# The output stage of an RWKV block: the bonus moved into the scan, the head norm from one root

## The reference, cut to what matters

```python
ym = jnp.mean(y, -1, keepdims=True)                    # per token and head
yv = jnp.mean(jnp.square(y - ym), -1, keepdims=True)
y = ((y - ym) * lax.rsqrt(yv + RW_LNX_EPS)).reshape(B, L, D) * lnx_g + lnx_b
kd = kf[None] * (1.0 + (a - 1.0) * k_a)                # a = sigmoid(a0 + la), both directions
kdh = (kd[0] + kd[1]).reshape(B, L, H, N)
bonus = jnp.sum(rh * kdh * r_k, -1, keepdims=True) * v
out = ((y + bonus.reshape(B, L, D)) * g)
return jnp.einsum('bld,de->ble', out, w_o)
```

## Time and profile before

| | us |
|---|---|
| median of 3 runs | 3148.36 (3147.19 to 3151.6) |
| profiled execution, its own time | 3148.75 |
| its span, first to last instruction | 3146.9 |
| TensorE busy | 2713.0 (86%) |
| VectorE busy | 2072.8 (66%) |
| ScalarE busy | 1583.4 (50%) |
| GpSimd busy | 436.3 (14%) |
| scan, in the span | 673 to 1020 |
| output stage up to the first matmul of `rw_o` | 1021 to 1116 |

### The profile page before, as it was taken

One profiled execution on the slowest core, in us unless ns is written; L12 is line 12 of the kernel. 1 busy time (PEld: TensorE's weight loads), 2 busy tenths in 40 slices (PEclk: granted clock), 3 DMA queues, 4 the chain that ended last, 5 costly groups with the idle time before them and its releaser, 6 DMA issues.

```text
span 3146.9 us, 58272 instructions
## 1 busy us (share of the span) xinstructions
PE 2713.0 (86%) x25152; PEld 2497.2 (79%) x25152; DVE 2072.8 (66%) x3070; ACT 1583.4 (50%) x2567; POOL 436.3 (14%) x271
## 2 busy tenths in 40 slices
PE   7868995848999468999999999999485788887898
PEld 7538995738999258999999999999483588886898
DVE  4664336774322457999999999999545567346683
ACT  3334433444111426777777777777343355344452
POOL 2002431111000110000000000000041134221242
PEclk9758997857988678999999999999787699988999
DMA  5103451200000126999999999999131134431353
GB/s 217 45 17 115 171 186 48 82 24 3 4 4 6 72 83 227 359 341 342 357 341 352 346 337 369 334 352 357 68 127 58 41 140 169 148 136 59 128 179 117
DMA packets 83209, 539.38 MB, mean 171 GB/s; under 512 B 9488, under 2 KB 9488, under 8 KB 38912
## 3 DMA queue, kind: packets, MB, share of 16 engines
q1 hardware_dynamic: 82368, 530.99, 45.9%
q0 software_dynamic: 576, 4.58, 0.4%
HBM read 534.49 MB, written 1.05 MB: 170 GB/s over the span
## 4 chain that ended last, share of the span: by engine, by line
PE 70%; DVE 19%; ACT 8%; issue 1%; DMA 1%; POOL 1%; DVEq 0%; SPq 0%; ACTq 0%; POOLq 0%
PE ps L557 18%; PE ps L558 17%; PE ps L559 17%; DVE sl L512 2%; ACT sh L505 2%; PE ps L1255 2%; DVE arena_conv L2596 2%; PE ps L563 2%; DVE xl L553 1%; PE ps L602 1%; PE ps L1259 1%; ACT xh L548 1%; PE ps L1248 1%; PE ps L1223 1%; PE ps L1706 1%
## 5 line engine op out<-in xcount | busy, mean ns | idle before, releaser
L1926 DVE TENSOR_TENSOR sl<-ring,sh 128x1024 fp32r<-128x1024 f32 x613 | 735.0, 1219 | 29.9 <-ACT sh L1884 18.8
L557 PE MATMUL ps<-xh,sh 128*128 128x256 f32 (+1 forms) x1888 | 574.5, 304 | 134.2 <-DVE xl L553 89.9
L1884 ACT ACTIVATE sh<-ring 128x1024 fp32r<-128x1024 f32 x613 | 630.4, 1053 | 3.1 <-DVE xl L1766 1.9
L557 PE MATMUL ps<-sh,xh 128*128 128x256 f32 (+2 forms) x2012 | 594.5, 295 | 13.6 <-POOL sl L519 6.0
L558 PE MATMUL ps<-sl,xh 128*128 128x256 f32 (+2 forms) x2012 | 574.9, 286 | 0.0
L559 PE MATMUL ps<-sh,xl 128*128 128x256 f32 (+2 forms) x2012 | 574.4, 286 | 0.0
L558 PE MATMUL ps<-xl,sh 128*128 128x256 f32 (+1 forms) x1888 | 562.1, 298 | 0.0
L559 PE MATMUL ps<-xh,sl 128*128 128x256 f32 (+1 forms) x1888 | 558.4, 296 | 0.0
L519 POOL TENSOR_TENSOR sl<-ring,sh 128x1024 fp32r<-128x1024 f32 (+3 forms) x111 | 273.6, 2465 | 1953.0 <-ACT sh L505 1892.5
L557 PEld LDWEIGHTS ps<-xh,sh 128*128 128x128 f32 x1888 | 379.6, 201 | 158.3 <-DVE xl L553 102.1
L505 ACT ACTIVATE sh<-ring 128x1024 fp32r<-128x1024 f32 (+1 forms) x345 | 342.3, 1021 | 182.6 <-PE ps L559 163.1
(11 more groups left out here) (514 smaller groups left out, 4436.2 us busy)
## 6 DMA issues: line engine op xcount, KB each, us to landing
ring<-ws_d SPq DMA_DIRECT2D x229, 1024.0 KB, 7.2
ring<-ws_d SPq DMA_DIRECT2D x80, 1536.0 KB, 6.4
ring<-ws_d SPq DMA_DIRECT2D x226, 512.0 KB, 6.8
ring<-ws_d SPq DMA_DIRECT2D x24, 1408.0 KB, 6.0
ring<-ws_d SPq DMA_DIRECT2D x4, 1256.0 KB, 5.4
ring<-ws_d SPq DMA_DIRECT2D x2, 1088.0 KB, 5.0
scan_t<-scn_d POOLq DMA_DIRECT2D x1, 1824.0 KB, 7.7
arena<-ow_d POOLq DMA_DIRECT2D x1, 1536.0 KB, 12.1
```

What stands on the lines that cost most here:

```text
L557: e.matmul(out, ah, bh, start=start, stop=False)
L1884: e.activation(out, raw(u)[:, a:z], ACT.Copy).then_inc(*af.on("high", u, i))
L1926: e.tensor_tensor(l, raw(u)[:, a:z], f32(h), SUB).then_inc(s_fd if i < 2 else s_fp, 1)
```

## The change

The bonus leaves the output stage. It becomes a third generator of the scan, on every engine, which joins after the second direction's set-up and two further rounds; each of its eight tiles takes four rounds: a2's two matmuls and two sigmoids, GpSimd's two operations, VectorE's two products and TensorE's head sum, and VectorE's product with v. It reads a2's weights from the scan's constants, so `ow_d` is 1 MB, and writes into `KK`, whose content is used up by then (`VV = KK`). In the output stage the mean is taken off by one matmul with I - ones/64 (`centre`); ScalarE squares out of PSUM, VectorE writes the centred values times the gain; eight matmuls with 16 columns (`heads64`) sum the squares of all 16 heads into 16 rows of one bank; one addition, one root and one reciprocal on 16 rows follow; then for each tile the gate's matmuls, and two matmuls (K = 16, 64 columns each) that spread two heads' scales over their 64 partitions, and on VectorE scale, bias plus bonus, gate, and the low part of the tile before. TensorE waits for `ow_d` only ahead of the first gate. The constants grow by 158 columns. The loops over `staged(8, 5)` in the four output programs, which are printed above, are taken out.

```diff
+    c.append(("centre", 128, lambda _: (np.eye(128) - blk / 64).astype(f)))
+    head_of = (np.arange(30)[None, :] - 14 == p[:, None] // 64).astype(f)
+    c.append(("heads64", 30, lambda _: head_of / f(64)))
...
 def out_weights():
     return [("g2", D, lambda inp: inp["rw_g2"][0, 0:128]),
-            ("g2b", D, lambda inp: inp["rw_g2"][0, 128:160]),
-            ("a2", D, lambda inp: np.reshape(inp["rw_a2"][0], (128, D)))]
+            ("g2b", D, lambda inp: inp["rw_g2"][0, 128:160])]
...
         PREPARE = 6
-
-        def streams(steps):
+        VV, va1 = KK, HW
+        def streams(steps, bonus):
             runs = [steps(n) for n in range(2)]
             for _ in range(PREPARE):
                 next(runs[0])
+            for _ in range(PREPARE + 2):
+                for g in runs:
+                    next(g)
+            runs.append(bonus())
             while runs:
                 runs = [g for g in runs if next(g, "end") != "end"]
...
+            def bonus():
+                for k in range(8):
+                    for n in range(2):
+                        b, free = psum.take(("out a", n, k))
+                        w.wait_ge(*free)
+                        e.matmul(PS[:, b, 0:T0], sn("a2")[64 * n:64 * n + 64, 128 * k:128 * k + 128], HA[64 * n:64 * n + 64, :], start=True, stop=True).then_inc(
+                            *pe.on("out a", n, k))
+                    yield
+                    yield
+                    yield
+                    colsum_pe(w, e, ("quad", k), "blk", VV[:, k:k + 1, :], 1, T0, dv["quad", k])
+                    yield
+            streams(steps, bonus)
...
+            def bonus():
+                for k in range(8):
+                    for n, v in ((0, VV[:, k, :]), (1, va1)):
+                        w.wait_ge(pe["out a", n, k], dv["prepared", 1, 1], *([po["out b", k - 1]] if n and k else []))
+                        e.activation(v, PS[:, psum["out a", n, k], 0:T0], ACT.Sigmoid, bias=par(f"a0{n}")[:, k:k + 1]).then_inc(*ac.on("out a", n, k))
+                        psum.gone["out a", n, k] = [ac.now()]
+                    for _ in range(4):
+                        yield
+            streams(steps, bonus)
...
+            def bonus():
+                for k in range(8):
+                    va = VV[:, k, :]
+                    yield
+                    yield
+                    w.wait_ge(po["out a", k])
+                    e.scalar_tensor_tensor(out=va, in0=va, scalar=2.0, in1=Kr[:, k, :], op0=ADD, op1=MUL).then_inc(*dv.on())
+                    w.wait_ge(dv.now())
+                    e.scalar_tensor_tensor(out=va, in0=va, scalar=par("r_k")[:, k:k + 1], in1=Rr[:, k, :], op0=MUL, op1=MUL).then_inc(*dv.on("quad", k))
+                    yield
+                    yield
+                    w.wait_ge(pe["quad", k], dv.now())
+                    e.tensor_tensor(va, PS[:, psum["quad", k], 0:T0], Vr[:, k, :], MUL).then_inc(*dv.on("bonus", k))
+                    psum.gone["quad", k] = [dv.now()]
+            streams(steps, bonus)
...
+            def bonus():
+                for k in range(8):
+                    yield
+                    va = VV[:, k, :]
+                    w.wait_ge(ac["out a", 1, k])
+                    e.tensor_tensor(va, va, va1, ADD).then_inc(*po.on("out b", k))
+                    w.wait_ge(po.now())
+                    e.tensor_scalar(va, va, -2.0, par("k_a")[:, k:k + 1], ADD, MUL).then_inc(*po.on("out a", k))
+                    for _ in range(3):
+                        yield
+            streams(steps, bonus)
...
-        VB, VV = at(tail_o + nw, 3, T0), at(tail_o + nw + 3 * T0, 3, T0)
-        SM, VA = (cut(scan_t, 2 * SLOTS * BW + i * XW, 8, T0) for i in (1, 3))
+        rs = at(tail_o + nw, T0)
+        YG, SQ = (cut(scan_t, 2 * SLOTS * BW + i * XW, 8, T0) for i in (1, 3))
...
         def out_pe(w, e):
-            w.wait_ge(*bar("scan"), IN_OW)
-            for j, k in staged(8, 5):
...
+            w.wait_ge(*bar("scan"))
+            for k in range(8):
+                b, free = psum.take(("centred", k))
+                w.wait_ge(*free, IN_CON)
+                e.matmul(PS[:, b, 0:T0], con("centre"), Yb[:, k, :], start=True, stop=True).then_inc(*pe.on("centred", k))
+            b, free = psum.take(("y var",))
+            w.wait_ge(*free)
+            for k in range(8):
+                w.wait_ge(ac["y square", k])
+                last = e.matmul(PS[0:16, b, 0:T0], con("heads64")[:, 14 - 2 * k:30 - 2 * k], SQ[:, k, :], start=k == 0, stop=k == 7)
+            last.then_inc(*pe.on("y var"))
+            for k in range(8):
+                b, free = psum.take(("gate", k))
+                w.wait_ge(*free, IN_OW)
+                e.matmul(PS[:, b, 0:T0], wo("g2", k), HG, start=True, stop=False)
+                e.matmul(PS[:, b, 0:T0], wo("g2b", k)[0:32, :], HG2[0:32, :], start=False, stop=True).then_inc(*pe.on("gate", k))
+                b, free = psum.take(("y scale", k))
+                w.wait_ge(*free, dv["y scales"])
+                for p in range(2):
+                    last = e.matmul(PS[64 * p:64 * p + 64, b, 0:T0], bc(con("ident")[0:16, 2 * k + p:2 * k + p + 1], 64), rs[0:16, :], start=True, stop=True)
+                last.then_inc(*pe.on("y scale", k))
             linear_pe(w, e, "rw_o", x_ro, T0)
...
-            for j, k in staged(8, 5):
-                if j == 0:
...
+            for k in range(8):
+                w.wait_ge(pe["centred", k])
+                e.activation(SQ[:, k, :], PS[:, psum["centred", k], 0:T0], ACT.Square).then_inc(*ac.on("y square", k))
+            w.wait_ge(dv["y eps"])
+            e.activation(rs[0:16, :], rs[0:16, :], ACT.Sqrt).then_inc(*ac.on("y root"))
+            for k in range(8):
+                w.wait_ge(dv["gated", k])
+                high_part(e, x_ro, k, Yb[:, k:k + 1, :])
             for i in tiles["rw_o"]:
...
-            for j, k in staged(8, 5):
-                y, va = Yb[:, k, :], VA[:, k, :]
...
+            for k in range(8):
+                w.wait_ge(ac["y square", k], IN_PAR)
+                e.tensor_scalar(YG[:, k, :], PS[:, psum["centred", k], 0:T0], par("lnx_g")[:, k:k + 1], None, MUL).then_inc(*dv.on("y by g", k))
+                psum.gone["centred", k] = [dv.now()]
+            w.wait_ge(pe["y var"])
+            e.tensor_scalar(rs[0:16, :], PS[0:16, psum["y var",], 0:T0], 64e-5, None, ADD).then_inc(*dv.on("y eps"))
+            psum.gone["y var",] = [dv.now()]
+            w.wait_ge(ac["y root"])
+            e.reciprocal(rs[0:16, :], rs[0:16, :]).then_inc(*dv.on("y scales"))
+            for k in range(8):
+                y, yg = Yb[:, k, :], YG[:, k, :]
+                w.wait_ge(pe["y scale", k], dv.now())
+                e.tensor_tensor(yg, yg, PS[:, psum["y scale", k], 0:T0], MUL).then_inc(*dv.on())
+                psum.gone["y scale", k] = [dv.now()]
+                w.wait_ge(dv.now())
+                e.scalar_tensor_tensor(out=y, in0=yg, scalar=par("lnx_b")[:, k:k + 1], in1=VV[:, k, :], op0=ADD, op1=ADD).then_inc(*dv.on())
+                w.wait_ge(dv.now(), pe["gate", k])
+                e.tensor_tensor(y, y, PS[:, psum["gate", k], 0:T0], MUL).then_inc(*dv.on("gated", k))
+                psum.gone["gate", k] = [dv.now()]
+                if k:
+                    low_part(w, e, x_ro, k - 1, Yb[:, k - 1:k, :])
+            low_part(w, e, x_ro, 7, Yb[:, 7:8, :])
             for n, i in enumerate(tiles["rw_o"]):
                 split_low(w, e, i)
                 w.wait_ge(pe["rw_o", n])
...
-            for j, k in staged(8, 5):
-                if j == 1:
...
```

More of the change, by code:

```diff
@@ L1300, in steps @@
                     yield
-            streams(steps)
+            def bonus():
[11 more added lines that the diff above has]
+            streams(steps, bonus)
             pe.mark("scan")
@@ L1592, in out_pool @@
             split_low_pool(w, e, "rwkv out")
-            for j, k in staged(8, 5):
-                if j == 1:
-                    va = VA[:, k, :]
-                    w.wait_ge(ac["out a", 1, k])
-                    e.tensor_tensor(va, va, VB[:, k % 3, :], ADD).then_inc(*po.on("out b", k))
-                    w.wait_ge(po.now())
-                    e.tensor_scalar(va, va, -2.0, par("k_a")[:, k:k + 1], ADD, MUL).then_inc(*po.on("out a", k))
             for i in tiles["rw_o"]:
```

## The result

The changed kernel takes 3117.05 us, median of 4 runs (3114.96 to 3117.14), against 3148.7 before, measured beside it. The ratio is 0.9897, with a 95% interval of 0.988 to 0.9914: 31.7 us or 1.0% faster. 3108 was forecast, in a range of 3092 to 3134. The profiled execution took 3117.05 us itself, with a span of 3115.2 (3146.9 before), so the spans differ by the same 31.7.

The account below looks back on a forecast made before the run. TensorE was taken to bound the scan, and no engine the output stage, a ring of handoffs. From 3148.75 us, -53.6 (output stage) - 2 (`rw_o`) + 15 (bonus in the scan) gave 3108, range 3092 to 3134.

Parts of the forecast that it names:

- part 1: Output stage's start: centring costs nothing, covered by the block's load and ScalarE's split; variance sum starts at 1032.8.
- part 2: Output stage, one norm for 16 heads: sums of squares 8.7 us, then addition, root and reciprocal 2.9, to 1044.4.
- part 3: Output loop over tiles: full clock, 2.3 us a tile, 18.4 for eight; `rw_o` starts at 1062.8, gain 53.6 us.
- Rival (a): Output loop runs at 1.2 GHz: 33 us instead of 18.4, no gain in `rw_o`, about 3125; chance 0.20.
- part 4: `rw_o` would begin at the full clock: 26.8 becomes about 24.8 us, gain 2.
- part 5: Bonus in the scan: TensorE has no idle time there, so its work lengthens the scan; cost 15 us, between 8 and 30.
- rival (b): In the scan, head sums wait for products and the clock falls behind them: 35 us more, 3143; chance 0.12.
- (c): The scan's whole bonus stretch, 115 us, falls to 1.2 GHz: 95 us more, 3203; chance 0.04.
- The sum: Whole kernel: output stage -53.6, `rw_o` -2, scan +15, together -40.6 us, so 3108.1.
- the forecast's own neighbourhood: Whole kernel's time between 3099 and 3117 us, given a chance of 0.52.

Follow-up runs that it names:

- dead matmuls' run: 14 overwritten matmuls before the first centring one, added to the changed kernel with bonus in 64 by 64 quarters and full-shape output loop; 3093.09 us, ratio 0.9818.
- gate-ahead run: The changed kernel with the second tile's gate matmuls issued ahead of the first spreading pair; 3116.55 us, ratio 0.989.
- run with one shape: The changed kernel with all output-loop matmuls at full 128 by 128, by zero rows and one spreading matmul; 3112.8 us, ratio 0.9886.

## Why the prediction was right, and where its steps were off

**The start (part 1)** held. Centring is covered; sums of squares begin 11.8 us behind the scan's end, forecast 12.4. The dead matmuls' run shows that the cover is real: 6.5 us more work there delayed nothing.

**One norm (part 2)** was a little dear: 11.6 forecast, 8.4 measured, because the clock rose within the sums (5.58 us for the eight). The root and the reciprocal had the lengths forecast, 0.43 and 1.84.

**The loop over tiles (part 3)** is the step that failed. "I take the full clock from about 1044, and 2.3 us" gave 18.4; it took 24.2 (1060.76 to 1084.97) at PEclk 0.54. The spreading pair came in below its lower bound of 0.75: 0.22 us of loads and 0.41 behind them at the full clock, 0.29 and 0.81 at half; its two column halves run beside each other. The Trainium skill, TensorEngine Tiling (Array Packing), section Key Properties, states that different tiles work in parallel, and these rows agree. The clock was the error. I counted TensorE as unbroken and therefore fast. The profile does count it as busy (24.0 of 24 us), yet behind every change of shape it loads nothing for 0.7 us. Rival (a) named this outcome at a fifth of the chance, for two reasons: short work broken by shape changes, and a gap just before the loop. The gate-ahead run speaks against the gap, and the run with one shape bears out the first, with the padding's share in it open. Its 33 us were too dear for the 24.2, because a tile took 3.5 us and not 4.1.

**`rw_o` (part 4)** gained nothing (27.1 for 26.8), for the same reason: it again began at 1.2 GHz.

**The bonus in the scan (part 5)**: 15 forecast, 20.2 measured, 18.5 of it the bonus's, within the bounds of 8 and 30. The visits were sized about right: 13.7 us forecast, 14.6 by the estimate above. The share at 1.2 GHz was too small: 1.3 forecast, some 4 by that estimate. TensorE's waits for the bonus were 0.6 us in all, so rival (b) did not come. Nor did (c): the clock stayed low for 38 us of the bonus's 122 and then rose by itself, with the wide visits going on. But (c) took the falls to end within some 7 us, and the first one lasts 14 in the kernel before.

**The sum.** -53.6 - 2 + 15 became -51.6 + 0.3 + 20.2. The stage's gain came nearly as forecast only because two errors met, the loop's 5.8 us too few and the sums' and start's 3.8 too many. The result, 3117, lies inside the range of 3092 to 3134, at the upper edge of the forecast's own neighbourhood; of the 8.9 us by which the gain fell short, the loop and `rw_o` make 8.1 and the scan 5.2, less those 3.8 and 0.6 that lie behind. The loop, `rw_o` and half of the scan's miss are one mistake: shape changes were priced as gaps alone, not with the clock that goes with them.

## What to carry to other kernels

A few wide matmuls set among many narrow ones can cost more than their number suggests; here 16 visits cost 18.5 us, and 5.3 in the neighbours' shape. So try that shape, by cutting a block matrix into its quarters or by padding with rows of zeros, even if that means more or larger matmuls. Before counting on the fast clock, look whether the stretch changes shape, not only whether TensorE is shown as busy, and read the granted clock there: a change every 1.2 us went with 1.2 GHz, ten wide visits in 70 us left 2.4 GHz standing. And where a staged loop is a ring of handoffs, work that leaves it saves its latency in every turn, so it may pay to move it into a stage whose engine is full.

## What the runs showed that I had not expected

- TensorE stayed at 1.2 GHz through 24 us in which the profile shows no idle time, when each tile changed the array's shape three times; with one shape and zeros for padding, behind the same pause, it stood at 2.4 GHz. In the scan a low of 14 us became one of 38 with the wide visits, and the eleven after it ran at 2.4 GHz.
- Two matmuls of 16 rows and 64 columns each, on the two column halves, cost what one of 128 by 128 does: 0.22 us of weight loads and 0.67 of matmuls for both, against 0.30 and 0.72.
- VectorE's operation on SBUF operands doubled, 0.50 to 1.09 us, beside a subtraction of GpSimd's of 0.77. Its operations that read PSUM did not run beside it, so nothing is shown of them.
- One kernel's runs spread by 0.4% with a landmark moved by 9 us: a step of this size is more safely read in the trace than in the median of four.
